# The last feed-forward chunk of a two-block transformer kernel computed with its weights standing in the array

## What is computed

```python
def swiglu(x, w_gate, w_up, w_down):
    return (jax.nn.silu(x @ w_gate) * (x @ w_up)) @ w_down

f1 = swiglu(rms_norm(x, ffn1_pre_g[l]), ffn1_w_gate[l], ffn1_w_up[l], ffn1_w_down[l])   # D_FF = 2816
x = x + FFN_RESIDUAL_WEIGHT * rms_norm(f1, ffn1_post_g[l])
```

## Time and profile before

| | us |
|---|---|
| median of 3 runs | 998.54 |
| lowest, highest | 998.02, 1412.37 |
| the profiled execution, its own time | 998.26 |
| its span, first to last instruction | 996.5 |

### The profile page before, as it was taken

How to read it: one execution, slowest core, us unless ns; L and a number is a source line. 1 busy time by engine, 2 the same in 40 slices (tenths; PEclk the granted TensorE clock), 3 DMA queues, 4 the chain that set the end, 5 groups by cost and what they waited for, 6 DMA issues and landing times.

```text
span 996.5 us, 14601 instructions
## 1 busy us (share of the span) xinstructions
PE 991.7 (100%) x5303; PEld 834.5 (84%) x5303; DVE 709.3 (71%) x822; ACT 488.4 (49%) x614; POOL 209.3 (21%) x205
## 2 busy tenths in 40 slices
PE   9999999999999999999999999999999999999998
PEld 6888888878888888888888888888888888888887
DVE  6876767775788767676874588987876767666664
ACT  6444443664665534444544464466545445334342
POOL 2232322014100222223010071151000012223230
PEclk9999999999999999999999999999999999999999
DMA  9655656745424655565746554444537356555561
GB/s 310 225 172 184 206 185 206 269 129 190 126 88 168 202 177 202 177 205 175 243 158 189 191 170 139 158 143 153 163 104 240 127 173 231 172 186 194 184 209 43
DMA packets 116937, 178.53 MB, mean 179 GB/s; under 512 B 5792, under 2 KB 73920, under 8 KB 116768
## 3 DMA queue, kind: packets, MB, share of 16 engines
q1 hardware_dynamic: 115952, 174.86, 53.5%
q0 software_dynamic: 640, 1.42, 0.5%
q10 hardware_dynamic: 304, 1.70, 0.5%
HBM read 176.88 MB, written 2.64 MB: 180 GB/s over the span
## 4 chain that ended last, share of the span: by engine, by line
PE 98%; DVE 1%; DMA 0%; issue 0%; ACT 0%
PE acc L632 11%; PE acc L635 11%; PE acc L636 11%; PE tp L823 10%; PE gu L823 10%; PE gu L826 5%; PE tp L826 5%; PE tp L632 4%; PE tp L636 4%; PE tp L635 4%; PE gu L632 4%; PE gu L635 4%; PE gu L636 4%; PE acc L1102 1%; PE acc L911 1%; PE tp L682 1%
## 5 line engine op out<-in xcount | busy, mean ns | idle before, releaser
L1935 DVE TENSOR_TENSOR wlo<-raw,whi 128x2048 fp32r<-128x2048 f32 x140 | 329.0, 2359 | 153.6 <-ACT whi L1304 152.8
L1304 ACT ACTIVATE whi<-raw 128x2048 fp32r<-128x2048 f32 x150 | 285.8, 1908 | 62.0 <-PE acc L636 27.4
L823 PE MATMUL tp<-act_in,whi 128*128 128x512 f32 x432 | 103.0, 391 | 0.0
L823 PE MATMUL gu<-act_in,whi 128*128 128x512 f32 x432 | 102.6, 390 | 0.0
L1843 POOL TENSOR_TENSOR tmp<-tmp 128x256 f32<-128x256 f32 x54 | 39.7, 735 | 282.1 <-DVE tmp L2056 282.1
L1845 POOL TENSOR_TENSOR sil<-sil,tmp 128x256 f32<-128x256 f32 x54 | 88.7, 1643 | 33.5 <-ACT sil L1375 33.5
L823 PEld LDWEIGHTS gu<-act_in,whi 128*128 128x128 f32 x432 | 80.9, 188 | 16.6
L632 PE MATMUL acc<-whi,hT_hi 128*128 128x512 f32 x240 | 94.1, 392 | 0.1
L635 PE MATMUL acc<-wlo,hT_hi 128*128 128x512 f32 x240 | 93.7, 390 | 0.0
L636 PE MATMUL acc<-whi,hT_lo 128*128 128x512 f32 x240 | 93.4, 389 | 0.0
L823 PEld LDWEIGHTS tp<-act_in,whi 128*128 128x128 f32 x432 | 79.7, 188 | 16.1 <-issue 0.4
(11 more groups left out here) (364 smaller groups left out, 1818.5 us busy)
## 6 DMA issues: line engine op xcount, KB each, us to landing
raw<-in_w_in SPq DMA_DIRECT2D x96, 512.0 KB, 4.6
raw<-in_down SPq DMA_DIRECT2D x66, 512.0 KB, 4.1
raw<-in_gate SPq DMA_DIRECT2D x64, 512.0 KB, 4.4
raw<-in_up SPq DMA_DIRECT2D x64, 512.0 KB, 4.9
raw<-in_w_out SPq DMA_DIRECT2D x16, 512.0 KB, 4.7
raw<-in_w_branch_hg SPq DMA_DIRECT2D x8, 512.0 KB, 4.4
raw<-in_w_branch_attn SPq DMA_DIRECT2D x8, 512.0 KB, 4.7
post<-in_post_gains SPq DMA_DIRECT2D x3, 512.0 KB, 5.9
```

The lines of the kernel that those rows point to most:

```text
L823: pe.matmul(banks[:, a, :], w_hi[:, i, a * P:(a + 1) * P], both, start=i == 0, stop=False)
L1304: act.activation(split_weights(k)[0], raw[:, k % RING, :], ACT.Copy).then_inc(hi_ready, 1)
L1935: dve.tensor_tensor(w_lo, raw[:, k % RING, :], w_hi.bitcast(F32), ALU.subtract).then_inc(lo_ready, 1)
```

## The change

The last chunk takes the `features` form for its gate and up pieces. The pieces are loaded as in the loop (a whole gate piece, then a whole up piece, instead of two pieces of half gate and half up); the four `half` calls and the turning of `hid` go. The last chunk's `hid` goes through the two sums, the two POOL multiplications and silu like that of a chunk of the loop, and its high part and remainder are written into the same places of `act_in` as before. Between the up product and down 10 of tile 0 stands down 9 of tile 0, as before. On DVE the remainder of the up piece moves within the loop from the end of one pass to the next pass, behind the gate sums.

```diff
-                for j in range(2):
-                    gate_up(f, k + j, 0, NC - 1, j)
+                gate_or_up(wg_d[f], k, 0, NC - 1)
+                gate_or_up(wu_d[f], k + 1, 0, NC - 1)
...
                 pe.wait_ge(gate_sum, s0 + 2 * (NC - 2))
-                half(k, 0, tp, 0, 0)
-                half(k + 1, 0, tp, 1, 0).then_inc(gu_first, 1)
-                half(k, 0, tp, 0, 1)
-                half(k + 1, 0, tp, 1, 1)
+                features(k, 0, tp)
                 pe.wait_ge(up_sum, s0 + 2 * (NC - 2))
-                turn_last(0)
+                features(k + 1, 0, gu)
                 pe.wait_ge(hT_lo_ready, t0 + 2 * NC - 3)
                 down(k + 2, 0, of_step, False, 0)
-                turn_last(1)
-                pe.wait_ge(hT_lo_ready, t0 + 2 * NC - 2)
                 last_down(k + 3, 0)
                 down(k + 2, 0, of_step, False, 1, ends=u_next is None)
-                pe.wait_ge(hT_lo_ready, t0 + 2 * NC - 1)
                 last_down(k + 3, 1)
...
                 hi(last)
-                edge_silu(last - 2, NC - 1, 0)
+                silu(NC - 1, 0)
+                silu(NC - 1, 1)
                 if n1 is not None:
                     hi(n1)
-                edge_silu(last - 2, NC - 1, 1)
-                for t in range(TT):
-
-                    if t and n1 is not None:
-                        hi(n1 + 1)
-                    act.wait_ge(hT_full, 3 * f + 2 + t)
-                    act.activation(last_hT(act_hi, t), heads(gu[:, t, 0:S], 2), ACT.Copy).then_inc(hT_hi_ready, 1)
+                act.wait_ge(piece_used, last - 1)
+                for a in range(2):
+                    act.wait_ge(h_ready, h0 + 2 * NC - 1 + a)
+                    act.activation(last_feature(act_hi, a), heads(hid[:, a, :], 2), ACT.Copy).then_inc(hT_hi_ready, 1)
+                if n1 is not None:
+                    hi(n1 + 1)
...
-                with pool.Fori(1, NC - 1) as c:
+                with pool.Fori(1, NC) as c:
...
-                lo(n0 + 7)
...
                         gate_parts(n0 + 5, c - 2, c, a)
-                    lo(n0 + 8, c - 2)
-                    lo(n0 + 9, c - 2)
+                    for n in range(7, 10):
+                        lo(n0 + n, c - 2)
                     up_parts(n0 + 7, c - 2, c, 0)
                     hidden(c, 0)
                     up_parts(n0 + 7, c - 2, c, 1)
                     hidden(c, 1)
-                    lo(n0 + 10, c - 2)
-                lo(n0 + 3 * NC - 1)
-                product(NC - 1, 0)
+                last = n0 + 3 * NC - 1
+                for a in range(2):
+                    gate_parts(last - 3, 0, NC - 1, a)
+                lo(last - 1)
+                lo(last)
+                for a in range(2):
+                    up_parts(last - 2, 0, NC - 1, a)
+                for a in range(2):
+                    dve.wait_ge(hT_hi_ready, t0 + 2 * NC - 2 + a)
+                    dve.tensor_tensor(last_feature(act_lo, a), heads(hid[:, a, :], 2), last_feature(act_hi, a).bitcast(F32),
+                                      ALU.subtract).then_inc(hT_lo_ready, 1)
                 if n1 is not None:
                     lo(n1)
-                product(NC - 1, 1)
-                for t in range(TT):
-                    dve.wait_ge(hT_hi_ready, t0 + 2 * NC - 2 + t)
-                    dve.tensor_tensor(last_hT(act_lo, t), heads(gu[:, t, 0:S], 2), last_hT(act_hi, t).bitcast(F32),
-                                      ALU.subtract).then_inc(hT_lo_ready, 1)
```

More of the change, by code:

```diff
@@ L421, in last_hT, with last_feature @@
             return h[:, 2 * t:2 * t + 2, P:2 * P]
+        def last_feature(h, a):
+            return h[:, 0:4, P:2 * P].rearrange("p (t a) n -> p a t n", a=2)[:, a, :, :]
         gate, row = tmp[:, 0, :].rearrange("p (a n) -> p a n", a=2), tmp[:, 1, 0:S]
@@ L790, in ffn @@
             def ffn(f, n0, u_next):
-                h0, s0, t0 = 2 * f * NC, 2 * f * (NC - 2), f * (2 * NC - 1)
+                h0, s0, t0 = 2 * f * NC, 2 * f * (NC - 1), f * (2 * NC - 1)
                 def turn_hidden():
@@ L798, in turn_hidden @@
                             mm = pe.transpose(turned_hid[:, a, t * P:(t + 1) * P], hid[:, t, a * P:(a + 1) * P], idn)
[L799 to L805, removed]
                     mm.then_inc(hT_full, 1)
@@ L856, in last_down @@
                         for a in range(2):
+                            if t == 0 and b == 0:
+                                pe.wait_ge(hT_lo_ready, t0 + 2 * NC - 2 + a)
                             mm = three(acc[:, t, b, :], *of_last(a, t), w_hi[:, a, b * BLK:(b + 1) * BLK],
@@ L1358, in ffn, with edge_silu @@
             def ffn(f, n0, n1):
-                h0, s0, t0 = 2 * f * NC, 2 * f * (NC - 2), f * (2 * NC - 1)
-                def edge_silu(k, c, t):
+                h0, s0, t0 = 2 * f * NC, 2 * f * (NC - 1), f * (2 * NC - 1)
+                def edge_silu(t):
                     if t == 0:
-                        act.wait_ge(gu_first, 2 * f + (2 if c else 1))
+                        act.wait_ge(gu_first, f + 1)
                     else:
[L1366 to L1369, removed]
+                        act.wait_ge(piece_used, n0 + 2)
+                    if f:
+                        act.wait_ge(h_ready, h0 - 1 + t)
+                    act.activation(sil[:, t, :], gu[:, t, 0:FC], ACT.Silu, scale=rstd[:, t:t + 1]).then_inc(sil_ready, 1)
                 def silu(c, a):
@@ L1382, in ffn @@
                 act.wait_ge(rstd_ready, norm_n(f"pre{2 * f}", 0))
-                edge_silu(n0 + 1, 0, 0)
+                edge_silu(0)
                 if f == 0:
@@ L1386, in ffn @@
                 act.wait_ge(rstd_ready, norm_n(f"pre{2 * f}", 1))
-                edge_silu(n0 + 1, 0, 1)
+                edge_silu(1)
                 hi(n0 + 3)
@@ L1393, in ffn @@
                 act.activation(row, turned_rstd, ACT.Copy).then_inc(rstd_row, 1)
-                act.wait_ge(hT_full, 3 * f + 1)
+                act.wait_ge(hT_full, f + 1)
                 act.activation(hT_hi[:, :, :], turned_hid, ACT.Copy).then_inc(hT_hi_ready, 1)
@@ L1835, in ffn @@
             def ffn(f):
-                h0, s0 = 2 * f * NC, 2 * f * (NC - 2)
+                h0, s0 = 2 * f * NC, 2 * f * (NC - 1)
                 pool.wait_ge(rstd_row, f + 1)
-                with pool.Fori(1, NC - 1) as c:
+                with pool.Fori(1, NC) as c:
                     for a in range(2):
@@ L2037, in ffn, with product @@
             def ffn(f, n0, n1):
[L2038 to L2047, removed]
+                h0, s0, t0 = 2 * f * NC, 2 * f * (NC - 1), f * (2 * NC - 1)
+                def product(t):
+                    dve.wait_ge(sil_ready, h0 + t + 1)
+                    dve.scalar_tensor_tensor(out=hid[:, t, :], in0=gu[:, t, FC:2 * FC], scalar=rstd[:, t:t + 1],
                                              in1=sil[:, t, :], op0=ALU.mult, op1=ALU.mult).then_inc(h_ready, 1)
@@ L2072, in hidden @@
                     dve.tensor_tensor(hT_lo[:, a, :], hid[:, a, :], hT_hi[:, a, :].bitcast(F32), ALU.subtract).then_inc(hT_lo_ready, 1)
-                product(0, 0)
-                product(0, 1)
+                product(0)
+                product(1)
                 lo(n0 + 3)
```

## The result

| | before | the change |
|---|---|---|
| median, us | 998.15 (8 runs) | 1001.38 (8 runs) |
| lowest | 997.91 | 1001.08 |
| the profiled execution's span | 996.5 | 999.4 |

The change is slower by 3.2 us: the ratio is 1.0035, with a 95% interval of 1.0026 to 1.0043. That is a third of a per cent, but clear of 1. The run of 1412.37 us is one of the eight before; the median is 998.15 with it and without it, and the ratio is formed without it.

The account below looks back on a forecast made before the run. PE, busy 100%, was taken as the bound. Two feed-forwards at +1.7, the third at +0.15 and the first loop pass at +0.15 gave +3.7 us on 998.26; with 0.28 added, the forecast was 1002.1 us, range 998.2 to 1004.2.

Parts of the forecast that it names:

- the case that it gave the highest chance: The forecast itself, 1002.1 us, from 1001 to 1003: late `hid`, then late `x`, no loop cost; chance 0.62.
- the 0.28: Amount by which the median of the runs shown stood above the profiled execution's 998.26 us, added to the sum.
- PE's own work: Last chunk on PE: fewer turns of `hid` but more matmul instructions, net -0.27 us per feed-forward, -0.8 for three.
- `hid`: At down 10 of tile 0, PE resumes at 493.4 instead of 492.03, waiting 1.4 us for the first remainder.
- `x`: At the turn of `x`: normalisation starts at 498.0 instead of 495.46; PE arrives at 499.6 and starts at 500.2.
- The third feed-forward: End of the last feed-forward, without a next stage's piece: PE resumes 0.45 us late; less 0.27 saved, +0.15.
- The loop: Ordinary passes: `hid` complete about 1.5 us before PE asks instead of 2.3, cost zero; rival that cover is lost, 0.05.
- the term for the first pass: First pass of the first feed-forward's loop, already waiting 0.2 us and without cover: +0.15 us.
- The unknown price: Whether a DVE up sum reading PSUM holds POOL up: forecast no; if so, up to 0.69 us per meeting.
- the rival that needed this: A sum holds POOL up as well: 0.5 us more in the first two feed-forwards, over 1 in the third; 1004.0, chance 0.13.
- the chain in time: Last chunk: POOL gets through beside the remainders and `hid` arrives at about 492.0 with PE; 998.4 us, chance 0.17.
- The bare saving: The change does only what it says on PE, with neither wait: 997.7 us, chance 0.03.

Follow-up runs that it names:

- the run with the piece between the silus: Against the change: ACT rounds the next stage's first piece between the last chunk's two silus instead of behind them; 1000.0 us, ratio 1.0017 to the kernel before.
- the form without the loop's part: Against the change: the up piece's weight remainder put back at the end of a loop pass; 1001.36 us, ratio 1.0033 to the kernel before.
- the run with `hid` first: Against the change: ACT rounds both halves of `hid` ahead of the next stage's first piece; 1006.16 us, ratio 1.0076 to the kernel before.

## Why the prediction was right

The forecast was 1002.1 us, the median is 1001.38, and the case that it gave the highest chance is the one that came, step by step. Start, sum and the 0.28 come to 1002.24, which it wrote as 1002.1. The 0.86 us by which that is above the median are 0.47 from the sum, nearly all from the first pass of the loop (below), and 0.39 from the start: three runs before had a median of 998.54, eight have 998.15.

- **PE's own work.** Forecast -0.27 per feed-forward. In the second, 1.36 + 0.53 were lost and the stretch grew by 1.62: -0.27. In the third 0.46 was lost and it grew by 0.26: -0.2. Right, and too little to pay for any wait.
- **`hid`.** On the prediction's clock PE resumed at 493.34; forecast 493.4. The way there was the forecast's: a first POOL scaling at its own pace, the next two held by DVE's remainders (1.69 and 2.78 us; of the four scalings only one lies in the 2 to 3 us that were named as the sign), the second product waiting for POOL, ACT's piece ahead of `hid`, 1.36 us lost (forecast 1.4). The run without the second multiplication shows POOL's part and the run with the piece between the silus ACT's; either is enough to take most of this loss away. That it is DVE's remainders that hold POOL rests on when the held scalings end and on the form without the loop's part, where one remainder stood there instead of two and one scaling was held instead of two. One detail was otherwise: the second remainder did not start 0.6 us late behind POOL, as forecast, but at once, and took 2.83 us; it ended at 489.58 on that clock, forecast 489.55.
- **`x`.** DVE began to normalise at 497.85 on that clock (forecast 498.0), PE turned `x` at 500.06 (forecast 500.2), 0.53 lost (forecast 0.6). The run with the second remainder behind the normalisation shows the cause.
- **The third feed-forward.** +0.26, forecast +0.15: the 0.46 that it lost was forecast as 0.45, and the saving was 0.2 instead of 0.27. PE's row there:

```profile
988.19 0.47 PE L636 MATMUL acc<-proj_rounded,act_in 128*128 128x512 f32 x1 [0.23 <-DVE act_in L2100]
```

- **The loop.** No wait of PE in it, as forecast, but the term for the first pass had the wrong sign: -0.31 instead of +0.15. It carried the later up sums of an ordinary pass over to the first. In the first pass the remainder stood ahead of four memsets and the first gate sums; DVE before and after, at the same place:

```profile
47.52 1.21 DVE L2056 TENSOR_REDUCE tmp<-tp 128x256 f32<-128x512 f32 x2
```

```profile
43.61 1.21 DVE L2045 TENSOR_REDUCE tmp<-tp 128x256 f32<-128x512 f32 x2
```

  With the remainder out of the way the gate sums came 3.9 us sooner, the first up sum at 54.86 instead of 56.20 (0.26 of either is that the first loop began earlier in this execution), and the first wait of the loop went. The 0.46 us between the two terms are nearly all by which the sum of +3.7 was too high against +3.23.
- **The unknown price.** The forecast took it that a sum from PSUM does not hold POOL. POOL's gate scaling ended at 491.24, 0.6 after the remainder that it had met, with an up sum running on DVE from 490.57: it lost nothing to the sum, and the rival that needed this is out. The gate sums show it as well: POOL's scaling at 484.82 took 0.74 us beside the sum of 485.01, and in the kernel before the one at 48.21 took 0.74 beside the gate sums of 47.52 to 48.73, so the price need not have been left open. The Trainium skill (SBUF — State Buffer, section Who interferes with whom) has it so: a `tensor_reduce` on DVE of this chip never contends with GpSimd, and an instruction with both inputs in SBUF contends with GpSimd's reads. The trace agrees on both: 0.74 us beside the sums, 1.69 and 2.78 beside the remainders.

The other rivals: the chain in time fell at the point named for it. It had the first remainder of `hid` at 492.0; that remainder started only at 492.77 on the prediction's clock, since the silu scaling and the second gate scaling were held. The loop kept its cover. The bare saving did not come even without POOL's second multiplication, because of DVE. The prediction's remark that a measurement of this kernel can hardly tell less than 2% from no change was too cautious: 0.35% came out clear.

## What to carry to other kernels

Where one engine is busy for 100%, a form that is cheaper on it by 0.25 us must be judged by what it puts on the others at that place: here four sums on DVE and four multiplications on POOL, two of them held, just where DVE has to split the next stage's weights as well and had 0.9 us to spare. A loop body is a poor guide to its last pass: in the loop the same chain has a whole piece of PE's work to hide behind, at the end half a one. And when a wait is taken away by a change of order on a full engine, look for the next thing in that engine's line: the orders tried here moved the wait between `hid`, the turn of `x` and the turned `x`, and none removed it.

## What the runs showed of the hardware that was not expected

- A wait costs PE more than the bracket in the timeline says: listed 1.12, 0.31 and 0.23 us were 1.36, 0.53 and 0.46 between starts, 0.2 more each. Why is not shown.
- In the run with `hid` first, after an idle stretch of PE of 2.0 us, the granted clock fell to 0.50 (1.2 GHz) for some 3 us, which cost a further 1.6 us, in the first two feed-forwards of the profiled execution; after 1.1 and 1.7 us of idle time in other kernels it stayed at 1.00. The runs don't show what decides it.
- The holding goes both ways: the remainder that began at 487.82 while POOL was still at work took 2.83 us, against 2.28 for the one before it.
